# A two-layer hybrid decoder step: one eviction moved behind the next block's correction, and a new order of score, transpose and value products in the mixer

## The reference, cut to what matters

```python
x = LN1(ALPHA * x + 0.5 * (silu(x @ wg1) * (x @ wu1)) @ wd1)
z = x @ w_in                       # 3 conv inputs, 2 LRU inputs, q, 3 gates
y_conv = (cb * conv3(cc * cv)) @ conv_out
y_lru  = (rg_lru(conv4(lx)) * gelu(lg)) @ lru_out
p      = softmax(q k_mem^T / sqrt(128))      # 4 heads, 256 memory tokens
y_att  = (p v_mem) @ att_out
m = (sigmoid(g0) * y_conv + sigmoid(g1) * y_lru + sigmoid(g2) * y_att) @ w_o
x = LN2(ALPHA * x + m)
x = LN3(ALPHA * x + 0.5 * (silu(x @ wg2) * (x @ wu2)) @ wd2)
```

## Time and profile before

| | |
|---|---|
| median of 3 runs | 1437.01 us (1436.47 to 1437.32) |
| the profiled execution | 1437.01 us, its span 1435.2 us |
| TensorE busy | 1412.7 us (98%) |
| VectorE busy | 898.7 us (63%) |
| ScalarE busy | 667.3 us (46%) |
| transfers | 243.62 MB, mean 170 GB/s |

### The profile page before, as it was taken

One profiled execution on the slowest core, in us unless ns is written; L12 is line 12 of the kernel. 1 busy time (PEld: TensorE's weight loads), 2 busy tenths in 40 slices (PEclk: granted clock), 3 DMA queues, 4 the chain that ended last, 5 costly groups with the idle time before them and its releaser, 6 DMA issues.

```text
span 1435.2 us, 25643 instructions
## 1 busy us (share of the span) xinstructions
PE 1412.7 (98%) x10680; PEld 1402.4 (98%) x10680; DVE 898.7 (63%) x1178; ACT 667.3 (46%) x893; POOL 29.3 (2%) x62
## 2 busy tenths in 40 slices
PE   7999999999999999999999999999999999999996
PEld 7999999999999999999999999999999999999996
DVE  4555568587655785554685555687866468755545
ACT  4444447344334674444474444463623346644433
POOL 1000000000000000000000000000000000000000
PEclk9999999999999999999999999999999999999999
DMA  7444444554545545454445454445455444544441
GB/s 255 174 175 153 158 166 168 207 184 169 193 175 172 176 151 180 167 175 162 162 162 178 173 175 156 167 164 174 155 213 183 159 155 146 190 157 174 167 163 55
DMA packets 39566, 243.62 MB, mean 170 GB/s; under 512 B 4528, under 2 KB 4544, under 8 KB 15808
## 3 DMA queue, kind: packets, MB, share of 16 engines
q1 hardware_dynamic: 32976, 219.30, 44.2%
q0 software_dynamic: 5936, 22.01, 4.3%
q10 hardware_dynamic: 576, 1.18, 0.2%
HBM read 238.97 MB, written 3.50 MB: 169 GB/s over the span
## 4 chain that ended last, share of the span: by engine, by line
PE 96%; DVE 2%; DMA 1%; issue 1%; ACT 0%; SPq 0%; DVEq 0%
PE ps L401 30%; PE ps L403 30%; PE ps L402 30%; PE ps L593 2%; PE ps L584 2%; DMA raw<-in_ffn_wu 1%; PE ps L487 1%; PE ps L559 1%; PE ps L599 1%; PE ps L615 0%; DVE wlo L980 0%; DVE y L1166 0%; DVE y L1160 0%; PE ps L431 0%; PE ps L432 0%
## 5 line engine op out<-in xcount | busy, mean ns | idle before, releaser
L980 DVE TENSOR_TENSOR wlo<-raw,whi 128x1024 fp32r<-128x1024 f32 x448 | 511.4, 1147 | 346.8 <-ACT whi L690 346.7
L690 ACT CAST whi<-raw 128x1024 fp32r<-128x1024 f32 x448 | 440.4, 986 | 514.8 <-PE ps L403 448.4
L401 PE MATMUL ps<-xh,whi 128*128 128x288 f32 (+1 forms) x2144 | 636.4, 297 | 1.2 <-DVE xl L1174 1.1
L402 PE MATMUL ps<-xl,whi 128*128 128x288 f32 (+1 forms) x2144 | 631.4, 295 | 0.0
L403 PE MATMUL ps<-xh,wlo 128*128 128x288 f32 (+1 forms) x2144 | 630.8, 294 | 0.0
L401 PEld LDWEIGHTS ps<-xh,whi 128*128 128x128 f32 x2144 | 404.3, 189 | 3.0 <-DVE xl L1174 1.6
L402 PEld LDWEIGHTS ps<-xl,whi 128*128 128x128 f32 x2144 | 405.7, 189 | 0.7
L403 PEld LDWEIGHTS ps<-xh,wlo 128*128 128x128 f32 x2144 | 405.3, 189 | 0.0
L401 PE MATMUL ps<-hh,whi 128*128 128x288 f32 (+1 forms) x1088 | 322.5, 296 | 0.0
L402 PE MATMUL ps<-hl,whi 128*128 128x288 f32 (+1 forms) x1088 | 319.3, 293 | 0.0
L403 PE MATMUL ps<-hh,wlo 128*128 128x288 f32 (+1 forms) x1088 | 319.1, 293 | 0.0
(11 more groups left out here) (178 smaller groups left out, 817.2 us busy)
## 6 DMA issues: line engine op xcount, KB each, us to landing
raw<-in_w_in SPq DMA_DIRECT2D x48, 1024.0 KB, 4.9
raw<-in_ffn_wu SPq DMA_DIRECT2D x44, 1024.0 KB, 4.8
raw<-in_ffn_wg SPq DMA_DIRECT2D x43, 1024.0 KB, 4.8
raw<-in_ffn_wd SPq DMA_DIRECT2D x32, 1024.0 KB, 4.9
raw<-in_ffn_wd SPq DMA_DIRECT2D x16, 768.0 KB, 4.2
pool<-in_cache_k POOLq DMA_DIRECT2D x16, 512.0 KB, 4.2
pool<-in_cache_v POOLq DMA_DIRECT2D x16, 512.0 KB, 5.0
raw<-in_w_o SPq DMA_DIRECT2D x8, 1024.0 KB, 5.1
```

Source lines behind the costliest of these rows:

```text
L401: mm(out, wh, mh, start=start, stop=False)
L402: mm(out, wh, ml, start=False, stop=False)
L690: s_.copy(whi[:, s, k0:k1, :], raw[:, s, k0:k1, :]).then_inc(hi_ready, 1)
L980: return v.tensor_tensor(out, full, high.bitcast(F32), sub)
```

## The change

There are three edits.

1. On ScalarE the eviction of the first fill leaves `norm`. In the Z stages it is now made in the loop over blocks, behind line 841's two instructions; it is the same eviction, and the loop makes no splits for it. In the FFN stages it is made in the first pair, behind the tanh and the two splits `hi_next(1, 0)` and `hi_next(1, 1)`, and ahead of the first copies of x.
2. On TensorE `prompt_scores(0)` comes behind the transposes of the sample scores, and not ahead of them.
3. The samples' probabilities are transposed into bank 5, which `prompt_transposes` uses too. So `prompt_transposes(0)` comes behind the wait for VectorE's copy (`spt_ready`), and `sample_values(0)` comes behind the projection block. The other heads keep their order.

```diff
-                prompt_scores(0)
                 pe.wait_ge(sst_ready, l + 1)
...
                     if i > 0:
                         pe.wait_ge(p_exp, l * (NT * AH) + NT * i)
-                        prompt_scores(i)
+                    prompt_scores(i)
                     gate(1, i)
                     if i == 0:
                         pe.wait_ge(s_prob, l + 1)
                         for m in range(MT):
-                            r = nc.tensor.transpose(ps[:, 7, m * P:(m + 1) * P], spr[:, m * P:(m + 1) * P], ident[:, :])
+                            r = nc.tensor.transpose(ps[:, 5, m * P:(m + 1) * P], spr[:, m * P:(m + 1) * P], ident[:, :])
                         r.then_inc(spt_psum, 1)
+                        pe.wait_ge(spt_ready, l + 1)
                     prompt_transposes(i)
+                    if i > 0:
+                        sample_values(2 * i)
+                    else:
+                        pe.wait_ge(b_ready, l + 1)
+                    project(1, i)
                     if i == 0:
-                        pe.wait_ge(spt_ready, l + 1)
-                        pe.wait_ge(b_ready, l + 1)
-                    sample_values(2 * i)
-                    project(1, i)
+                        sample_values(0)
                     prompt_values(i)
...
                             hi_next(1, 0)
                             hi_next(1, 1)
+                            for fill in gap(3 * l + 2 * f - 1):
+                                evict(*fill)
                             write_x(*divmod(3 * l + 2 * f - 1, 3), 0)
...
                     hi(third(n, q), 1)
-                    for fill in gap(q)[0:1]:
-                        evict(*fill)
                     act.wait_ge(scaled_first, q + 1)
...
-                for n, j, f in blocks[2:]:
+                for n, j, f in blocks[1:]:
                     if j is not None and j >= 8:
                         break
                     if f is not None:
                         evict(n, f)
-                    z_hi(n)
+                    if n > blocks[1][0]:
+                        z_hi(n)
...
-                        v.tensor_copy(spt[:, :, :], ps[:, 7, 0:MT * P].rearrange("p (t c) -> p t c", t=MT)).then_inc(spt_ready, 1)
+                        v.tensor_copy(spt[:, :, :], ps[:, 5, 0:MT * P].rearrange("p (t c) -> p t c", t=MT)).then_inc(spt_ready, 1)
```

## The result

The changed kernel takes 1450.22 us (median of 4 executions, 1446.02 to 1451.13), the kernel before 1437.16 us (median of 4 beside it). The ratio is 1.0087, 95% interval 1.0064 to 1.011. That is slower, as forecast, but by 13.1 us where 6.5 had been forecast, and 1450.22 lies outside the range of 1440.8 to 1445.8. The profiled execution took 1447.18 us, 10.2 more than that of before.

The account below looks back on a forecast made before the run. TensorE, busy for 98% of the 1435.2 us span, was taken to bound the kernel, so new waits add their whole length. 4.21 + 0 + 1.36 + 0.88 = 6.45 us on 1437.01 gave 1443.5 us, range 1440.8 to 1445.8.

Parts of the forecast that it names:

- Part 1: Z stages: the second fill waits for the late eviction to free its banks, stalls of 2.03 and 2.18 us, together 4.21.
- Part 2: Second FFN of layer 0, first of layer 1: the later eviction is covered, 0 us; 1.1 us if uncovered.
- Part 3: Mixer: without the prompt's scores as cover, TensorE waits for VectorE's copy of sample scores, 0.68 us, twice, 1.36.
- Part 4: Mixer: prompt transposes sharing bank 5 wait for VectorE's copy of sample probabilities, 0.44 us, twice, 0.88.
- Part 4, its last paragraph: Mixer: sample_values(0) behind the projection delays the next load of cached values to 397.4, wanted at 402.08: cost 0.
- Rival C: Z stages: TensorE returns at half rate from its 2 us stalls, 1.6 us each, twice 3.2; 1446.7 us; chance 0.06.
- A: Z stages: the late evictions cost nothing, only the mixer's 2.24 us remain; 1439.3 us; chance 0.06.
- B: Mixer: the new order gains, removing the 0.32 us stall before sample_values(0) and hiding L643's wait; 1440.6 us; chance 0.06.

Follow-up runs that it names:

- the run with two pairs of banks: Kernel before with only the late eviction in the Z stages, fills alternating between banks 6, 7 and banks 4, 5: 1437.38 us, ratio 1.0006.
- The kernel with the waits alone: Kernel before with the changed mixer order and shared bank 5, but sample_values(0) still ahead of the projection block: 1439.36 us, ratio 1.0016.
- the kernel with the order changed for all heads: Kernel before with sample_values(2 i) behind the projection block for all four heads, no new wait on the softmax: 1444.81 us, ratio 1.0053.
- the long run: Kernel before with only sample_values(0) moved behind the projection block, joining small products into one row of 5.2 us: 1437.55 us, ratio 1.0.
- the version that spreads them best: Kernel before with prompt_scores(i + 1) moved ahead of sample_values(2 i): 1435.64 us, ratio 0.9989.

## Why the prediction was wrong

**Part 1, the eviction and the bank: right.** 4.21 us forecast, 2.07 + 2.14 = 4.21 us measured as stops in the profile; the single stops are 0.04 us off, and that they cancel is luck. That the splits behind the eviction cost nothing fits the run with two pairs of banks, within 2 us.

**Part 2: right.** 0 forecast, +0.2 us with an interval around zero (-1.0 to +1.6 us).

**Part 3, the scores as cover: right.** Forecast 0.68 us for each layer, measured 0.63. In the changed profile L642 starts at 381.44, 0.06 us behind the end of VectorE's copy at 380.96 + 0.42 = 381.38.

**Part 4, the transposes behind the copy: right.** L606 starts 0.06 us behind VectorE's copy and the projection 0.39 us later (389.80 to 390.19), against 0.44; the loss measured in layer 1 is 0.42. The kernel with the waits alone, +2.5 us, has parts 3 and 4 in it, forecast at 2.24. The row that was preferred to the page's figure for a transpose (the Trainium skill, TensorE: Matmul & The Clock Gate, Part 4: PE-mode transpose) held: four transposes took 0.42 us and not 1.1.

**Part 4, its last paragraph: the step that failed, first half.** "Moving sample_values(0) behind the projection ... cost 0." Only the load of the cached values was looked at, and that was indeed covered. What was missed is what TensorE itself then does: 40 products of sample values, prompt values and scores in a row of over 5 us, with no large product between. The runs show that this row lowers the granted clock, without any wait (the kernel with the order changed for all heads, +7.8 us). The sum had no term for the clock at all: "whatever newly makes TensorE wait adds its whole length" took the length of a stop for its whole price.

**Rival C: the step that failed, second half.** It described what happened, half clock behind the stops in Z, and priced one fall right (1.6 us against 1.5), but got 0.06. The reason given against it, that the stop from 1217.24 to 1218.58 was followed by products at full pace, rests on one execution of a thing that happens in a share of executions, and on a stop of 1.2 us. It also counted two places, while the measured kernel had four or five in its profiled executions, the mixer's among them. The Trainium skill (TensorE: Matmul & The Clock Gate, Why this matters for your kernels) warns of idle gaps between bursts; this case agrees in kind, and shows falls behind gaps of 2 us and some with no gap at all. Over the seven executions of the changed kernel the clock took 12.8 us, in the kernel before 5.3. These 7.5 us more are 6.6 at 1.5 us a stretch, and with them the forecast of 6.45 comes to 13.1, against 13.1 measured.

**Rivals A and B: out.** Neither part came for free.

**Two slips in the numbers.** The chances of the forecast, B and C add up to 0.91 and not 0.92, and that of a gain is given as 0.03 and then as 0.02. The range is said to reach down to B, but B's 1440.6 us lies just below 1440.8. Neither touches the sum.

What stays open: what makes the clock fall at one place and not at the next of the same make; why the waits and the long run, each under 1 us of clock alone, take 4.1 us together; and how large each share of falls is, since only one execution of each kernel was profiled (two of the changed one) and the clock of the others is known to 0.001 of the span, about one fall.

## What to carry to other kernels

In a kernel that is bound by TensorE, count not only the stops that an edit makes but also how long a row of small products it puts together: gathering them cost up to 7.8 us with no wait in the profile, and the version that spreads them best, with no stop in the mixer either, had a clock of 0.997 or better in all 12 executions. Look for half-clock stretches by windows, and at several executions' clocks, because one clean profile does not show that a place is safe. An eviction that looks hidden on its own engine still owns the bank: before it is moved, look for the next writer, or give the writers two banks.

## What had not been expected of the hardware

The granted clock fell to 0.50 in pieces of 3.4 us or twice that, in the middle of stretches in which TensorE was busy throughout. By its clocks the kernel before has it as well in some executions, which is part of its spread from 1434.39 to 1440.61 us: the 11 executions at 0.995 have a mean of 1438.6 us, the 21 at 0.997 of 1435.9. The view by stretches has 1.00 for the kernel's first 12 us too, where the products are 0.24 us apart and not 0.13; the half pace at the start is in no mean clock here.

Large products also run at slightly different paces for whole stages, from one execution to the next, at a granted clock of 1.00. In the profile of the changed kernel:

```profile
30.00:200.00 170.00, 170.00 (x1293) 1.00 0.49 168
```

and in that of the kernel before:

```profile
30.00:200.00 170.00, 170.00 (x1288) 1.00 0.48 168
```

That is 0.4% fewer; in the window from 520 to 700 us the two have 1372 and 1369, nearly the same. The profiled execution of the changed kernel is some 2.7 us faster than its waits (6.3) and falls (6.2) say, against 9.8 us of span; the first of the two windows accounts for 0.7 us of it, and that the rest is pace too is an estimate. What sets the pace was not tried.
